# Prompt attention: another order of TensorE's work within a unit

## The reference

```python
o_cmp, p_cmp = attend_shared(q, ck, cv, cend[None, :] <= qpos[:, None])
...
o_sel = attend_gathered(q, k_sel, v_sel, kpos <= qpos[None, :, None, None])
...
o_win, _ = attend_shared(q, kw, vw, wmask)
o = gn[..., 0:1] * o_cmp + gn[..., 1:2] * o_sel + gn[..., 2:3] * o_win
```

## Time and profile before

| | |
|---|---|
| Runs, us | 2222.72, 2227.99, 2228.59; median 2227.99 |
| The profiled execution, us | 2222.76 (span 2220.8) |
| PE busy over the span | 2115.1 us, 95% |
| DVE, ACT, POOL busy | 927.9, 551.8, 616.5 us |
| Mean granted clock of TensorE | 0.982 |

### The profile page before, as it was taken

One profiled execution on the slowest core, in us unless ns is written; L12 is line 12 of the kernel. 1 busy time (PEld: TensorE's weight loads), 2 busy tenths in 40 slices (PEclk: granted clock), 3 DMA queues, 4 the chain that ended last, 5 costly groups with the idle time before them and its releaser, 6 DMA issues. The chain is left out here.

```text
span 2220.8 us, 38672 instructions
## 1 busy us (share of the span) xinstructions
PE 2115.1 (95%) x14076; PEld 1961.8 (88%) x14076; DVE 927.9 (42%) x1958; ACT 551.8 (25%) x1157; POOL 616.5 (28%) x545
## 2 busy tenths in 40 slices
PE   7999999888989999799999988999999999999997
PEld 6999999865855767599999977999999999999997
DVE  4111111176336676455661346563333333333435
ACT  5001211122326655222030332221111111111113
POOL 2233332345225444412212322212212122122221
PEclk9999999999979999899999999999999999999999
DMA  6112222385323000544212432111211112111112
GB/s 202 51 47 66 68 95 87 125 236 184 91 64 134 1 2 1 141 146 145 82 43 66 190 119 62 38 48 29 66 33 52 48 33 62 33 56 44 33 48 102
DMA packets 205798, 176.28 MB, mean 79 GB/s; under 512 B 26043, under 2 KB 184475, under 8 KB 205114
## 3 DMA queue, kind: packets, MB, share of 16 engines
q1 hardware_dynamic: 198298, 155.54, 22.9%
q0 software_dynamic: 5024, 10.69, 1.7%
q10 hardware_dynamic: 2368, 8.67, 1.0%
HBM read 147.55 MB, written 27.39 MB: 79 GB/s over the span
## 5 line engine op out<-in xcount | busy, mean ns | idle before, releaser
L191 PE MATMUL bank<-tail_hi,tail_w_hi 128*128 128x352 f32 x1248 | 403.3, 323 | 4.8 <-DVE tail_lo L407 3.7
L192 PE MATMUL bank<-tail_lo,tail_w_hi 128*128 128x352 f32 x1248 | 400.1, 321 | 0.0
L193 PE MATMUL bank<-tail_hi,tail_w_lo 128*128 128x352 f32 x1248 | 399.8, 320 | 0.0
L152 POOL TENSOR_TENSOR tail_w_lo<-mem_last_slot,tail_w_hi 128x1024 fp32r<-128x1024 f32 (+2 forms) x100 | 184.4, 1844 | 705.3 <-ACT tail_w_hi L140 705.3
L191 PE MATMUL bank<-mix_hi,in_w_hi 128*128 128x352 f32 x840 | 271.5, 323 | 0.0
L192 PE MATMUL bank<-mix_lo,in_w_hi 128*128 128x352 f32 x840 | 269.5, 321 | 0.0
L193 PE MATMUL bank<-mix_hi,in_w_lo 128*128 128x352 f32 x840 | 269.3, 321 | 0.0
L191 PEld LDWEIGHTS bank<-tail_hi,tail_w_hi 128*128 128x128 f32 x1248 | 234.1, 188 | 6.1 <-issue 5.7
L192 PEld LDWEIGHTS bank<-tail_lo,tail_w_hi 128*128 128x128 f32 x1248 | 234.5, 188 | 0.1
L193 PEld LDWEIGHTS bank<-tail_hi,tail_w_lo 128*128 128x128 f32 x1248 | 233.9, 187 | 0.0
L140 ACT CAST tail_w_hi<-mem_last_slot 128x1024 fp32r<-128x1024 f32 (+2 forms) x100 | 82.3, 823 | 526.3 <-PE bank L193 517.5
(11 more groups left out here) (383 smaller groups left out, 3514.5 us busy)
## 6 DMA issues: line engine op xcount, KB each, us to landing
in_raw<-w_in SPq DMA_DIRECT2D x70, 256.0 KB, 3.2
mem_last_slot<-w_gate SPq DMA_DIRECT2D x44, 256.0 KB, 3.2
mem_last_slot<-w_up SPq DMA_DIRECT2D x44, 256.0 KB, 3.2
mem_last_slot<-w_down SPq DMA_DIRECT2D x80, 128.0 KB, 2.2
gate_kept<-x_first ACTq DMA_DIRECT2D x16, 528.0 KB, 2.7
uv<-gate_kept SPq DMA_DIRECT2D x16, 528.0 KB, 4.6
mem_ring<-cache_mem_v SPq DMA_DIRECT2D x8, 1024.0 KB, 10.8
mem_ring<-cache_mem_k SPq DMA_DIRECT2D x7, 1024.0 KB, 10.4
```

Source lines behind the costliest of these rows:

```text
L152: pool.tensor_tensor(lo, raw, hi.bitcast(F32), ALU.subtract).then_inc(self.split, 1)
L191: pe.matmul(out, hi, x_hi, start=k == 0, stop=False)
L192: pe.matmul(out, hi, x_lo, start=False, stop=False)
L193: last = pe.matmul(out, lo, x_hi, start=False, stop=k == len(terms) - 1)
```

## The change

In PE's loop over the units, `values(u - 1)` moves between the first and the second turns of u, and `scores(u + 3)` moves behind the second turns. Nothing else is edited: every instruction, wait and buffer is as it was, and the programs of the other engines are unchanged.

```diff
                 for u in range(len(units)):
                     turn(u, 0)
+                    if u > 0:
+                        values(u - 1)
+                    turn(u, 1)
                     if u + 3 < len(units):
                         scores(u + 3)
-                    turn(u, 1)
-                    if u > 0:
-                        values(u - 1)
                 values(len(units) - 1)
```

## The result

| | before | changed |
|---|---|---|
| Median of the runs, us | 2227.22 | 2283.68 |
| Ratio, 95% interval | | 1.0265, 1.0249 to 1.0282 |
| Span of the profiled execution, us | 2220.8 | 2283.4 |
| Prompt attention, from its first matmul to the next stage's, us | 263.1 | 323.1 |

The change costs 2.65%, about 59 us (the medians above, which come from few runs, differ by 56). It lies in prompt attention: 632.12 to 895.26 before, 635.08 to 958.15 after, 60 us of the 62.6 by which the profiled spans differ. The forecast was 2270, 42 us more; sign and place were right, the size was short by some 30%.

The account below looks back on a forecast made before the run. The prediction took PE to bound the late tiles of prompt attention. Late tiles 34.8, early tiles 7 and the passage 1 summed to 43 us, 42 kept, giving 2270; range 2250 to 2288, with the clock's case 2244 to 2298.

Parts of the forecast that it names:

- The mechanism: Late tiles: VectorE's copy of second turns stands behind lower(u+3), which waits for late scores; PE goes on after 3.34 us.
- Values of the selected unit may start at 3.34: Tile 7, selected to window unit: scores and first turns end at 1.99, then PE stalls 1.35 us before values.
- The sign that was named: Tile 7's timeline: PE idles about 1.35 us before each selected unit's values, released by VectorE's copy.
- a step from selected to window unit: Tile 7, from selected to window scores: 6.24 us for 4.80 before; the window-to-selected step 6.30 for 5.20.
- Pairs: One selected plus one window unit: 10.04 us in tile 4, 11.39 in tile 5, 11.33 in tile 6, 12.54 in tile 7.
- once per late tile: Tiles 4 to 7 before the change: the wait for VectorE's copy already occurs once a tile, 0.97 us in tile 7.
- The sum: Prompt attention: late tiles 34.8, early tiles 7, passage from tile 3 to 4 1; 43 us, of which 42 kept.
- Tiles 4 to 7: Nine steps each: 43.8, 49.5 and 49.1 us in tiles 4 to 6; tile 7 up to the last scores 30.8.
- The 2 us that were to come back at the end: After the last scores: lower is gone, values stand where PE waited for copies before, so about 2 us come back.
- The early tiles: Tiles 0 to 3: GpSimd's normalising delays first turns, 0.3 to 0.9 us per pair, 7 us; passage to tile 4 one more.
- The clock's rival: Late tiles: PE's stalls also lower its clock, about +8 to +26 us, middle +17, 2287; chance 0.18.
- No change and faster: Two rivals: waits hidden, 2228; or late-tile stalls gone, 2222. Both need lower(u+3) within 2 us of scores; chance 0.04 each.

Follow-up runs that it names:

- experiment 1: Changed kernel, with VectorE copying a unit's second turns ahead of lower(u+3) instead of behind its first piece: 2241.11 us, ratio 1.0059 to the kernel before.
- Experiment 3: Changed kernel, with VectorE and ScalarE exchanging their copies, VectorE taking the odd groups: 2292.75 us, ratio 1.0283 to the kernel before.
- experiment 5: Kernel before, with new PE order in tiles 4 to 7 only; VectorE does lower(u+2) second piece, copy of u's second turns, lower(u+3) first piece: 2236.94 us, ratio 1.0052.
- experiment 8: The changed kernel run again unaltered, for a second profile: 2291.61 us.

## Why the prediction was right, and where it was not

**The mechanism held.** The copy of second turns behind lower(u+3), behind scores: 3.34 us from scores to release was read before, 3.35 is there after, and experiment 1 takes away most of the loss by moving that copy alone.

**The step that failed** is "Values of the selected unit may start at 3.34", with first turns hidden ahead of them. The next unit's first turns use the same two banks as the second turns that wait to be copied, so they wait too, and their own time comes after 3.34. The sign that was named, 1.35 us of idle time ahead of values, does not appear; 2.00 and 1.36 stand ahead of first turns instead. The row was at hand: in the earlier trace rows it is first turns that wait at 859.62. In tile 7 a step from selected to window unit became 6.83 for the 6.24 worked out, the other 6.61 for 6.30, since values now cover the later wait at second turns. Pairs: 13.44 for 12.54 in tile 7, 12.57 for 11.39 in tile 5. Experiment 3 shows the bank at work. A smaller misreading: "once per late tile" holds for VectorE's copy in tiles 5 and 7 alone; in tiles 4 and 6 of the kernel before the stall (0.78 and 0.77) is behind ScalarE's copy. The sum does not use it.

**The sum.** The stage grew by 59.9 where the terms came to 43. Tiles 4 to 7 took 1.1, 8.9, 1.6 and 1.8 more than worked out, the end, from the last scores on, 3.4. The 2 us that were to come back at the end are to be had: in experiment 1, with the same order of PE, the end takes 17.0 for 19.2 before. But the last scores too have a lower and a copy behind them, and first turns wait 2.00 for it (940.83), a wait that the sum left out there; 1.6 more is the clock. Of these 17 us, about 6 are the clock; the other 11, by subtraction, are first turns that wait, 2 of them at the end.

**The early tiles** had the right size by luck: 8 forecast, 8.2 in the changed kernel, 7.5 alone. GpSimd's normalising was the right engine to look at, but the loss was put in every pair. A pair of tile 3 lost 0.14 (726.63 to 733.40, before 720.11 to 726.74) for 0.3, one of tile 2 0.06 (698.42 to 704.04, before 690.71 to 696.27) for 0.6; the waits that grew lie at the compressed units.

**The clock's rival** had 0.18 and a price of 8 to 26. It came in a small form, 6.3 us, beside the forecast and not instead of it. The Trainium skill ("TensorE: Matmul & The Clock Gate", section "A second HAM failure mode: psum-queue depth-cycling") tells of a kernel whose PE idled for short times between groups, often enough that its clock swung. The trace agrees in part: 0.92 was granted in tile 5, where it was 1.00 before, but 1.00 in tile 4, where PE idled 9 of 45 us as well. The Trainium skill ("Trainium Kernel Development and Optimization", section "Performance Expectations") also names the share of weight loads, beside the share of the peak matmul rate, as what tells how near PE is to its limit. By that the waits could have been hidden; here they were not, each pair of tile 7 being 3.44 us longer, and the measurement decides.

**No change and faster** needed the copy done within 2 us of the scores; it took 3.2.

Left open: the other 3 us of experiment 3's excess over the changed kernel, why the clock fell where it did, and whether another order of ScalarE's loop would make experiment 5 the equal of the kernel before, which was not tried.

## What to carry to other kernels

An engine's place in a hand-written order is a contract with the other engines' programs: before a producer is moved back, look what stands behind its consumer in that consumer's own order, and whether the producer waits for that. Count a wait from the first instruction that needs the resource, here the PSUM bank of the next transposes, not from the one that needs the data.

## What was not expected of the hardware

Stalls of like size had unlike effects on the granted clock. In tile 5 a stall of 2.00 us at 804.14 came with 0.57 granted from 804 to 808, while the 2.00 of tile 7 at 913.96 left PE at its full pace (values in 1.90, as before). In the second profile the lower stretches sat at the same four steps (experiment 8).
